# mLSTM score products of one head in row pairs, with swapped copies of queries and context keys

## The reference

```
scores = einsum('bhtk,bhsk->bhts', qb, kb) * exp(log_w - m_t[..., None])
num    = w_inter[..., None] * einsum('bhtk,bhkv->bhtv', qb, C) + einsum('bhts,bhsv->bhtv', scores, vb)
den    = w_inter * einsum('bhtk,bhk->bht', qb, n) + sum(scores, -1)
h      = num / maximum(abs(den), exp(-m_t))[..., None]
```

## Time and profile before

| | us |
|---|---|
| three executions | 1689.84, 1692.56, 1705.3 (median 1692.56) |
| the profiled execution | 1690.28 |
| its span, first to last instruction | 1687.8 |
| PE busy | 1594.6 (94% of the span) |
| DVE busy | 788.0 (47%) |
| ACT busy | 698.7 (41%) |
| POOL busy | 202.9 (12%) |
| mean granted clock of TensorE | 0.974 of 2.4 GHz |

### The profile page before, as it was taken

The page is one execution under the profiler, slowest core; times in us unless marked ns, Lnnn a source line. Parts: engine busy times, 40 slices in busy tenths (PEclk is TensorE's granted clock), DMA queues, the critical chain, the costliest instruction groups (busy, mean ns, idle before and its releaser), DMA issues. The chain is left out here.

```text
span 1687.8 us, 24826 instructions
## 1 busy us (share of the span) xinstructions
PE 1594.6 (94%) x10526; PEld 1288.2 (76%) x10526; DVE 788.0 (47%) x1228; ACT 698.7 (41%) x996; POOL 202.9 (12%) x172
## 2 busy tenths in 40 slices
PE   5999999999999998899999999899999889989998
PEld 3888767765557776677777777688888658989998
DVE  4385236643633234532223232578276464565563
ACT  5623233354456233332113321452355656454452
POOL 0000002223001120121002200000013201112030
PEclk8999999989999999999999999999999999989999
DMA  8221322212031243155343444232232314435552
GB/s 347 103 101 51 131 88 113 94 55 94 32 112 57 88 157 132 47 201 195 139 186 143 181 148 177 75 131 73 90 132 79 123 63 142 144 146 209 192 175 100
DMA packets 36445, 212.82 MB, mean 126 GB/s; under 512 B 3888, under 2 KB 7344, under 8 KB 12656
## 3 DMA queue, kind: packets, MB, share of 16 engines
q1 hardware_dynamic: 36336, 211.24, 34.8%
HBM read 209.13 MB, written 2.10 MB: 125 GB/s over the span
## 5 line engine op out<-in xcount | busy, mean ns | idle before, releaser
L530 PE MATMUL ps<-parts,whi 128*128 128x512 f32 (+1 forms) x928 | 334.6, 361 | 10.7 <-DVE SQ L2021 6.4
L532 PE MATMUL ps<-parts 128*128 128x512 f32 (+1 forms) x960 | 332.2, 346 | 0.0
L1056 PE MATMUL ps<-parts 128*128 128x512 f32 (+1 forms) x960 | 323.1, 337 | 0.0
L531 PE MATMUL ps<-parts,whi 128*128 128x512 f32 (+1 forms) x928 | 321.0, 346 | 0.0
L1054 PE MATMUL ps<-parts 128*128 128x512 f32 (+1 forms) x928 | 315.3, 340 | 0.0
L1055 PE MATMUL ps<-parts 128*128 128x512 f32 (+1 forms) x928 | 312.6, 337 | 0.0
L1765 DVE TENSOR_TENSOR parts<-ring,parts 128x1024 fp32r<-128x1024 f32 x124 | 147.6, 1232 | 251.6 <-ACT parts L1342 251.6
L1342 ACT ACTIVATE parts<-ring 128x1024 fp32r<-128x1024 f32 x124 | 124.4, 1050 | 266.5 <-PE ps L1056 254.6
L1740 DVE TENSOR_TENSOR parts<-ring,whi 128x1024 fp32r<-128x1024 f32 (+1 forms) x136 | 165.0, 1255 | 114.8 <-ACT whi L1301 114.6
L530 PEld LDWEIGHTS ps<-parts,whi 128*128 128x128 f32 x928 | 177.2, 191 | 48.9 <-issue 26.8
L532 PEld LDWEIGHTS ps<-parts 128*128 128x128 f32 x960 | 183.0, 191 | 23.3
(11 more groups left out here) (266 smaller groups left out, 2080.5 us busy)
## 6 DMA issues: line engine op xcount, KB each, us to landing
ring<-in_w_ff SPq DMA_DIRECT2D x64, 1024.0 KB, 4.8
ring<-in_w_in SPq DMA_DIRECT2D x60, 1024.0 KB, 4.9
ring<-in_w_mod SPq DMA_DIRECT2D x40, 1024.0 KB, 4.8
arena<-in_w_mod SPq DMA_DIRECT2D x8, 1024.0 KB, 21.0
ring<-in_w_branch SPq DMA_DIRECT2D x32, 256.0 KB, 5.2
ring<-in_w_out SPq DMA_DIRECT2D x8, 1024.0 KB, 5.0
arena<-in_tables_rt SPq DMA_DIRECT2D x2, 1280.0 KB, 7.8
X<-in_x SPq DMA_DIRECT2D x2, 1024.0 KB, 8.1
```

Source lines behind the costliest of these rows:

```text
L530: pe.matmul(ps[0:m, 0:n], w_hi[:, k, c], x_hi[:, k, 0:n], start=(k == 0), stop=False)
L531: pe.matmul(ps[0:m, 0:n], w_hi[:, k, c], x_lo[:, k, 0:n], start=False, stop=False)
L532: last = pe.matmul(ps[0:m, 0:n], w_lo[:, k, c], x_hi[:, k, 0:n], start=False, stop=(k == KD - 1))
L1056: last = pe.matmul(ps[:, 0:nt], w_lo[:, k, c], x_hi[:, k, 0:nt], start=False, stop=(k == kt - 1))
```

## The change

`mlstm_scores` takes the place of `scores3`. ACT makes a copy of the latent queries and of the context keys in which the two halves of the partitions are exchanged: `LQ2` in unit 16 and `LK2` in unit 19 of the tile `arena`, which at that time nothing else uses. In the copies a head lies on the other 64 partitions (`far`) of the same plane. Bank 0 is then computed from `LK`, `LQ` on the head's own partitions (`near`) and bank 1 from `LK2`, `LQ2` on the others, a matmul of each in turn. Bank 2 (layer 0) is computed alone as before. Both banks of the pair are taken ahead of the first matmul. PE waits once for the copies, at head 0. `swap_halves` on ACT, four instructions of 64 partitions and 2 x 256 elements, stands between the evacuation of `rg` and `merge(l, HG, [0, 1])`.

```
+        LQ2, LK2 = [unit(i).rearrange("p (j t) -> p j t", j=2) for i in (16, 19)]
...
-            def scores3(key, l, k, q, h):
-
-                r = 64 * (h % 2)
-                for b in range(3 if l == 0 else 2):
-                    ps = bank((key, l, h, b))
-                    q0 = LAT if b == 2 else 0
+            def mlstm_scores(l, h):
+
+                near, far = [slice(64 * x, 64 * x + 64) for x in (h % 2, 1 - h % 2)]
+                j = h // 2
+                if h == 0:
+                    pe.wait_ge(*s_la.at(("swapped", l)))
+                pair = [bank(("lqk", l, h, b)) for b in range(2)]
+                for i in range(2):
+                    s = slice(i * P, (i + 1) * P)
+                    for ps, k, q in ((pair[0], LK[near, j, s], LQ[near, j, 0:LAT]), (pair[1], LK2[far, j, s], LQ2[far, j, :])):
+                        last = pe.matmul(ps[:, i * 256:(i + 1) * 256], k, q, start=True, stop=True)
+                        if i:
+                            last.then_inc(*product.up(("lqk", l, h, 0 if ps is pair[0] else 1)))
+                if l == 0:
+                    ps = bank(("lqk", l, h, 2))
                     for i in range(2):
-                        s = i if b == 0 else 2 + i
-                        last = pe.matmul(ps[:, i * 256:(i + 1) * 256], k[r:r + 64, h // 2, s * P:(s + 1) * P],
-                                         q[r:r + 64, h // 2, q0:q0 + LAT], start=True, stop=True)
-                    last.then_inc(*product.up((key, l, h, b)))
+                        s = LAT + i * P
+                        last = pe.matmul(ps[:, i * 256:(i + 1) * 256], LK[near, j, s:s + P], LQ[near, j, LAT:T],
+                                         start=True, stop=True)
+                    last.then_inc(*product.up(("lqk", l, h, 2)))
...
-                    scores3("lqk", l, LK, LQ, h)
+                    mlstm_scores(l, h)
...
+            def swap_halves(l):
+
+                act.wait_ge(*s_pa.at(("mk", l, 1)))
+                for o, i in ((LQ2, LQ[:, :, 0:LAT]), (LK2, LK[:, :, LAT:T])):
+                    for x in range(2):
+                        a, b = slice(64 * x, 64 * x + 64), slice(64 - 64 * x, P - 64 * x)
+                        last = act.activation(o[a], i[b], ACT.Copy)
+                last.then_inc(*s_la.up(("swapped", l)))
...
                 for j in range(2):
                     evac(l, "rg", j)
+                swap_halves(l)
                 merge(l, HG, [0, 1])
                 mlstm(l)
```

## The result

| | before | changed |
|---|---|---|
| median of 12 executions, us | 1690.03 | 1682.63 |
| lowest and highest | 1685.57 to 1705.3 | 1681.21 to 1684.37 |
| the profiled execution, us | 1690.28 | 1682.58 |
| its span | 1687.8 | 1680.7 |
| its mean granted clock | 0.974 | 0.979 |

The ratio is 0.9943, with a 95% interval of 0.9922 to 0.9965: 0.4 to 0.8% faster. By the medians the gain is 7.4 us where 4.0 was forecast. 2.5 of the 6.0 us come from the starting point: the forecast took off from the median of three executions, 1692.56, and the twelve have 1690.03. The other 3.4 us are gain that was not forecast. Two things are to be explained: whether the 4 us came as worked out, and where 3 more come from.

The account below looks back on a forecast made before the run. PE, with no idle time in the mLSTM stage, was taken to bound the kernel. Savings of 0.9 + 0 + 3.1 = 4.0 us gave 1686.3 us against the profiled execution, 1688.6 as a median, range 1683 to 1698.

Parts of the forecast that it names:

- starting point: Whole kernel: the profiled 1690.28 us less 4.0, plus 2.28 for the median of three runs, gives 1688.6 us.
- Price of a pair: mLSTM scores on PE: eight paired records save a head 0.85 us, 0.9 at head 0 of layer 0.
- Layer 0, heads 1 to 3: Layer-0 mLSTM stage: the 0.85 us a head become PE's wait at the gate product; 0 us saved, bounds 0 and 0.1.
- The bank wait: Layer 0, heads 1 to 3: the gate product's bank is free only after DVE's 12 distance instructions; gate starts 0.11 us later.
- Layer 1: Layer-1 mLSTM stage: heads 0, 1 and 3 keep 0.85 us, head 2 keeps 0.57; 3.1 us, bounds 2.0 and 3.8.
- The copies: Four ACT instructions a layer, 2.3 us, covered by ACT's idle time of 5.02 and 3.72 us: cost 0.
- After the stage: Behind the mLSTM stages: a shift of the last values carries through; the sum is 4.0 us.
- a rival with 0.15: Layer 0's new idle times at gate products lower the granted clock: +1.1 or +6.2 us, up to 1698.8; chance 0.15.
- everything is kept: Both mLSTM stages: no bank wait at the gate, all eight heads save 0.85 to 0.94: -7 us, 1685.6; chance 0.12.

Follow-up runs that it names:

- e8: The changed kernel with layer 0's third score products put behind each head's first gate product: 1680.85 us, against 1683.90 of the changed kernel in the same group.
- e11: The kernel before with pairs only in heads 1 to 3 of layer 0: 1689.88 us, ratio 1.0004 to the kernel before.
- e13: The kernel before with pairs only at head 0 of layer 0: 1686.56 us, ratio 0.9964 to the kernel before.
- e1: The changed kernel with copies and PE's wait kept, but the score products of the kernel before: 1691.37 us, ratio 1.0009 to the kernel before.
- e12: The kernel before, unchanged, profiled once more: a single execution of 1700.35 us with a clock of 0.974.
- e2: The changed kernel with pairs only in layer 0, copies in both layers: 1685.85 us, ratio 0.9955 to the kernel before.
- e3: The changed kernel with pairs only in layer 1, copies in both layers: 1686.89 us, ratio 0.9975 to the kernel before.
- e10: The kernel before with four matmuls (0.9 us) left out of the first gate product behind layer 0's head 0 scores: 1688.21 us, ratio 1.0003.
- e7: The changed kernel with the third score products of layer 0's head 0 made twice (+0.93 us): 1689.87 us, ratio 1.0000 to the kernel before.
- e4: The changed kernel with bank 1's two matmuls following bank 0's instead of taken in turn: 1683.35 us, ratio 0.9944 to the kernel before.

## Why the prediction was wrong

**Price of a pair: right.** 0.85 us a head were forecast from retention's rows, 0.9 for head 0 of layer 0. Measured: 0.86 us at head 0 of layer 0, and 1.92 - 1.06 = 0.86 us in layer 1.

**Layer 0, heads 1 to 3: right.** They keep nothing. The bank wait was worked out from the order of takings and a distance of 0.11 us between two engines. It came as 0.85 us of idle PE, and e8 took it away by putting the third product behind the gate product, which then takes another bank. e11 and e13 show it from the other side.

**Layer 1: right.** Forecast 3.1 us, measured 3.17. Head 2 was held by the probabilities as forecast; 0.06 us lie between them and the values, forecast 0.1.

**The copies: right** in that they cost 0 (e1); 2.55 us against 2.3 in length.

**The step that failed is "After the stage": the sum stopped at 0.9 + 0 + 3.1 = 4.0 us.** It took the granted clock of the profiled execution as given and put what the clock gives back at nothing. A gain of one or two stretches stood only in the low end of the range (1683), without a chance of its own; as a loss the clock had a rival with 0.15. That loss did not come. In the changed kernel's profile the stage, with its three new idle times, is at full clock throughout:

```profile
254.00:333.00 79.00, 76.40 (x433) 56.44 (x432) 50.14 (x113) 30.16 (x29) 20.38 (x19) 1.00 0.25 89
```

**The starting point was off as well.** To the profiled 1690.28 us the forecast added 2.28, for the median of three executions. The median of twelve is 1690.03, so 1690.03 - 4.0 = 1686.0 us would have been the same sum from the better start. The sentence that this measurement can't tell a change within 1% from none was wrong too: the interval of the ratio, 0.9922 to 0.9965, lies wholly below 1.

The missing term has two parts.

One is the long executions. 34 of 129 executions of before have a low clock, none of 24 of the changed kernel. Where a profile caught such a long one (e12, e1), its stretches lay in the layer-0 stage; of the others only the mean clock is known. The median of all 129 is 1690.09, that of the 95 others 1689.6, so this explains 0.5 us of a median and nearly all of the tail of before, from 1693 to 1706 us (27 of 30 such executions). The one profile at hand for the forecast did not show it: its clock in the stage was 1.00. The spread of the three executions did: 1705.3 beside 1689.84 was there to be asked about, and was put down to scatter.

The other is outside the stages. 1689.6 - 1683.05 (the median of 24 executions of the changed kernel) = 6.5 us, of which 4.0 are in the stages. About 2.5 us remain, and their cause stays open. By the medians they come with layer 0's head 0 (e2, e13 against e3, e11). The profiles don't bear that out: outside the stages the changed kernel has 1051.07 us in one and 1053.11 in the other, while e3 and e10, without head 0's pair, have 1051.62 and 1051.51. The shift by itself (e10) didn't bring them in the median, and the same shift undone (e7) cost more than it should. Each of these two has 12 executions spread over 13 us or more, and one or two profiles a kernel are too few to tell how often the short form comes.

**The rival "everything is kept"** would have given 1685.6 us, nearest to what was measured, for the wrong reasons: three heads did not keep their gain, and it started 2.5 us too high.

## What to carry to other kernels

Before forecasting a change on the busiest engine, write down the order in which it takes its PSUM banks and look for the reader that frees the bank some products on. A distance of 0.1 us between that reader's end and the engine's next product means that nothing ahead of it can be gained; moving one product behind it may free it (e8). Where executions of a kernel spread far more upwards than downwards, ask for the granted clock of each: they can carry a loss that one profile doesn't show. And before a few microseconds outside the changed place are put down to the change, take a second profile of each kernel and compare them between idle times that both have: here the same kernel differed by 2 us where nothing had been changed.

## What the runs showed of the hardware

- TensorE fell to 1.2 GHz while busy, for stretches of 6.80 and 13.60 us (e12). The stretches began within single-half products and values of 65 columns, 19 us and more behind the last idle time. Idle times of 0.85 to 0.90 us ahead of three gate products did not lower it in the changed kernel's profile (clock 1.00 from 254 to 333 us).
- Products on the two halves of the partitions overlap when two of one half are followed by two of the other (e4): 8 records of 64x256 in 1.14 us, as in turns. On one half, in single file, 8 take 1.99 us.
- ScalarE copies of 64x512 fp32 elements within on-chip memory, from one half of the partitions to the other, take 2.55 / 4 = 0.64 us each; one of 32x512 from PSUM takes 0.57.
- Four single-half records between dense products take 1.06 us (e8), while behind a pair they add 256.75 - 255.80 = 0.95 us.
